# Heads' norm reordered: three centring products first, three panels of the output projection begun together, three activation table loads placed earlier

## What is computed

```python
def rwkv7_time_mix(...):                       # layer 0
    ...
    y = scan over time                         # per head of 64 columns
    mean = jnp.mean(y, axis=-1, keepdims=True)
    var = jnp.mean(jnp.square(y - mean), axis=-1, keepdims=True)
    y = ((y - mean) * lax.rsqrt(var + LNX_EPS)).reshape(B, S, BR_W) * lnx_w + lnx_b
    return y + bonus

for l in range(DEPTH):                         # DEPTH = 2
    ...
    y = concat([y_br * silu(gate),             # 768 columns
                y_mem * silu(g_mem)]) @ w_out[l]   # 256 columns; w_out is 1024 x 1024
    x = x + rms_norm(y, post_norm[l])

# second block: two feed-forward parts around a mixer, then the final norm
h = h + 0.5 * swiglu(rmsnorm(h, ffn1_norm), ...)
h = h + hybrid_mixer(rmsnorm(h, mix_norm), ...)
h = h + 0.5 * swiglu(rmsnorm(h, ffn2_norm), ...)
y = rmsnorm(h, final_norm)
```

## Time and profile before

| | before |
|---|---|
| median of 3 runs | 1286.67 us (1284.4 to 1289.2) |
| profiled execution: its own time | 1287.15 us |
| span in the profile | 1285.3 us |
| granted TensorE clock, mean | 0.978 of full speed |
| busy: PE, DVE, ACT, POOL | 93%, 66%, 49%, 15% of the span |
| DMA | 186.83 MB, 145 GB/s on average |

### The profile page before, as it was taken

How to read it: one execution, slowest core, us unless ns; L and a number is a source line. 1 busy time by engine, 2 the same in 40 slices (tenths; PEclk the granted TensorE clock), 3 DMA queues, 4 the chain that set the end, 5 groups by cost and what they waited for, 6 DMA issues and landing times.

```text
span 1285.3 us, 23942 instructions
## 1 busy us (share of the span) xinstructions
PE 1197.6 (93%) x9724; PEld 1152.2 (90%) x9724; DVE 845.7 (66%) x1456; ACT 627.4 (49%) x1079; POOL 187.6 (15%) x186
## 2 busy tenths in 40 slices
PE   5978699898996899999999999989999999999997
PEld 5978688797996799999989999879999999999996
DVE  4768854776776686654497746669556668866642
ACT  5675352664555654444343445453445445654442
POOL 1127140200002021110022000015000001212101
PEclk8989799999998999999999999999999999999999
DMA  6434210344452565555336432335454345755560
GB/s 225 130 117 132 83 67 34 98 136 145 132 164 83 177 213 179 177 159 173 115 123 190 164 132 87 110 115 196 156 179 159 120 160 168 258 185 186 169 182 33
DMA packets 53677, 186.83 MB, mean 145 GB/s; under 512 B 6720, under 2 KB 8896, under 8 KB 53184
## 3 DMA queue, kind: packets, MB, share of 16 engines
q1 hardware_dynamic: 53008, 183.07, 43.8%
q10 hardware_dynamic: 560, 2.24, 0.5%
HBM read 184.24 MB, written 1.05 MB: 144 GB/s over the span
## 4 chain that ended last, share of the span: by engine, by line
PE 75%; DVE 14%; ACT 7%; issue 3%; DMA 1%; POOL 0%; DVEq 0%; SPq 0%; ACTq 0%; POOLq 0%
PE bank L2534 20%; PE bank L2537 20%; PE bank L2535 20%; DVE wl L1979 4%; ACT wh L1607 2%; PE bank L2551 2%; PE bank L2568 2%; PE bank L2552 1%; PE bank L2555 1%; DVE sqr L2083 1%; DVE zl L2079 1%; PE bank L2577 1%; ACT L1585 1%; DVE tmp L2447 1%; DVE score L2378 1%
## 5 line engine op out<-in xcount | busy, mean ns | idle before, releaser
L1979 DVE TENSOR_TENSOR wl<-raw,wh 128x1024 fp32r<-128x1024 f32 (+1 forms) x343 | 422.5, 1240 | 206.3 <-ACT wh L1607 202.7
L2534 PE MATMUL bank<-xh,wh 128*128 128x256 f32 (+1 forms) x1880 | 544.2, 289 | 1.8 <-ACT wh L1607 1.6
L2537 PE MATMUL bank<-xh,wl 128*128 128x256 f32 (+1 forms) x1880 | 535.7, 285 | 6.9 <-DVE wl L1979 6.9
L2535 PE MATMUL bank<-xl,wh 128*128 128x256 f32 (+1 forms) x1880 | 536.7, 285 | 0.0
L1607 ACT ACTIVATE wh<-raw 128x1024 fp32r<-128x1024 f32 (+1 forms) x343 | 355.2, 1044 | 273.3 <-PE bank L2537 258.3
L2537 PEld LDWEIGHTS bank<-xh,wl 128*128 128x128 f32 x1880 | 358.4, 191 | 8.3 <-DVE wl L1979 8.3
L2534 PEld LDWEIGHTS bank<-xh,wh 128*128 128x128 f32 x1880 | 356.6, 190 | 7.3 <-issue 3.6
L2535 PEld LDWEIGHTS bank<-xl,wh 128*128 128x128 f32 x1880 | 357.4, 190 | 0.5
L2534 PE MATMUL bank<-hh,wh 128*128 128x272 f32 (+1 forms) x352 | 100.3, 285 | 0.0
L2535 PE MATMUL bank<-hl,wh 128*128 128x272 f32 (+1 forms) x352 | 100.2, 285 | 0.0
L2537 PE MATMUL bank<-hh,wl 128*128 128x272 f32 (+1 forms) x352 | 100.2, 285 | 0.0
(11 more groups left out here) (376 smaller groups left out, 1726.2 us busy)
## 6 DMA issues: line engine op xcount, KB each, us to landing
raw<-w_ffn_gate SPq DMA_DIRECT2D x44, 512.0 KB, 3.6
raw<-w_ffn_up SPq DMA_DIRECT2D x44, 512.0 KB, 3.6
raw<-w_a_w_in SPq DMA_DIRECT2D x29, 512.0 KB, 3.6
raw<-w_ffn_down SPq DMA_DIRECT2D x32, 448.0 KB, 3.4
raw<-w_w_out SPq DMA_DIRECT2D x16, 512.0 KB, 3.5
raw<-w_b_w_in SPq DMA_DIRECT2D x16, 512.0 KB, 4.6
raw<-w_ffn_down SPq DMA_DIRECT2D x16, 512.0 KB, 3.6
raw<-w_ret SPq DMA_DIRECT2D x16, 512.0 KB, 3.9
```

The lines of the kernel that those rows point to most:

```text
L1979: v.tensor_tensor(lo[:, c], raws[n % N_RAW][:, c], hi[:, c].bitcast(F32), ALU.subtract).then_inc(*w_lo.up(n))
L2534: pe.matmul(ps, hi[:, c], x_hi(k), start=(k == 0), stop=False)
L2535: pe.matmul(ps, hi[:, c], x_lo(k), start=False, stop=False)
L2537: last = pe.matmul(ps, lo[:, c], x_hi(k), start=False, stop=(k == kt - 1))
```

## The change

In layer 0 the three `norm_a` steps come first, then `norm_b(0)`, then the group of the projection's panels on tiles 6 and 7, now three panels where there were two, then `norm_b(1)`, `branch0` 0, `norm_b(2)`, `branch0` 1 and 2. The memory pair's split (`branch0` 3) moves into `step_y(1)`, behind its third tile. In layer 1 the group keeps two panels. A new step `ln_tables` loads the Ln/Exp set ahead of `mix_out(1)`, and ahead of the last projection (`down`) of each of the two feed-forward parts.

```diff
+OUT_BEGUN = (3, 2)
             def begin_out(layer, part):
-                return begin([(f"w_out{layer}", panel, f"y{layer}", S, out_evac(layer)) for panel in range(2)], part)
+                return begin([(f"w_out{layer}", panel, f"y{layer}", S, out_evac(layer)) for panel in range(OUT_BEGUN[layer])], part)
                 finish(begun)
-                for panel in range(2, KT):
+                for panel in range(OUT_BEGUN[layer], KT):
                     do("y", c, i, b, freed)
                     bank.give(b, (yd, (c, i)))
+                    if c and i == 2:
+                        do("branch0", 3)
-            do("branch0", 3)
-            da0 = norm_a(0)
-            begun = begin_out(0, (6, 7))
-            norm_b(0, da0)
-            da1 = norm_a(1)
-            norm_b(1, da1)
-            da2 = norm_a(2)
-            do("branch0", 0)
-            norm_b(2, da2)
-            do("branch0", 1)
+            centred = [norm_a(j) for j in range(3)]
+            for j, da in enumerate(centred):
+                norm_b(j, da)
+                if j:
+                    do("branch0", j - 1)
+                else:
+                    begun = begin_out(0, (6, 7))
             do("branch0", 2)
             do("branch", BT + 1)
+            do("ln_tables")
             mix_out(1, begun)
+                do("ln_tables")
                 for panel in range(KT):
                     if panel == KT - 3:
                         fewer_splits()
                     project(f"ffn{n}_down", [panel], f"hid{n}", FFN_TOK[n], down_evac, kt=FT, keep=True)
+                elif kind == "ln_tables":
+                    tables(ACT.Ln)
```

## The result

| | before | after |
|---|---|---|
| median | 1287.45 us (10 runs, 1284.1 to 1291.7) | 1292.87 us (10 runs, 1290.4 to 1295.9) |
| ratio after/before, 95% interval | | 1.0043 [1.0028, 1.0058] |
| profiled execution, its span | 1287.15, 1285.3 | 1295.35, 1293.5 |
| mean granted clock | 0.978 | 0.973 |

The changed kernel is slower by 5.4 us. The prediction was 1288.1 with a range to 1291.3, so it was 4.8 us low and the time lies outside the range.

The account below looks back on a forecast made before the run. Taken as PE-bound nearly everywhere (75% of what ended last). Norm and projection +3.5, layer 1 load -1.0, final load -1.1 gave +1.4 us: 1288.6 against the profiled 1287.15, hence 1288.1 us median; range 1283.5 to 1291.3.

Parts of the forecast that it names:

- Ln 0 early: Heads' norm, ACT: the first Ln starts at about 227.71 instead of 228.52, 0.8 us early.
- the stop inside the group until DVE's `wl2`: Heads' norm, PE: after 8 of 18 matmuls the group stands from 231.0 to 232.4, delaying the sums of pairs 1 and 2.
- the shared tiles: Layer 0 projection: three panels sharing the remaining tiles take 7.8 us instead of 9.0, giving 1.2 us back.
- the pause ahead of panel 3: Layer 0 projection: panel 3's weight split, formerly hidden by panel 2, is uncovered and costs 1.6 us.
- `mo_add` straight behind DVE's `wl`: Layer 1's projection: without the table load there, `mo_add` follows DVE's `wl` directly, winning 1.0 us.
- the final Ln: Final norm: with the table load moved, Ln starts 0.03 us behind PE's last sum, winning 1.1 us.
- The drain: Skill page's estimate: about 1380 ns more per table switch, making two loads worth up to 5.3 us; left out of the sum.
- the 3.15 us late start of tile 0: Layer 0 projection, PE: tile 0 starts at about 238.9 instead of 235.75.
- the other 10 in 1.2 us: Heads' norm, PE: the group's last ten matmuls, once `wl2` is ready, take 1.2 us, ending at 233.6.
- the clock falls earlier: Rival, chance 0.12: PE's clock drops to 1.2 GHz at 232.4, slowing ten matmuls and sum 1; 1.8 us more, 1289.9.
- Later, the same pieces shifted by 3.5: Behind the norm and projection: the program's later pieces run as before, only 3.5 us later.
- shifts here pass on one for one: Behind layer 0's projection: a shift moves everything after by the same amount, since PE works without a pause.

Follow-up runs that it names:

- run 8: The changed kernel again, unaltered, for a second profile; 1292.74 us (1 run).
- run 11: The kernel before with six more Ln of 128x512 on ACT ahead of the first head's own Ln; 1297.55 us, ratio 1.0061.
- run 15: The kernel before with two more Ln of 128x512 ahead of the first head's own; 1295.41 us, ratio 1.0051.
- run 14: The changed kernel with two begun panels, transposes filling PE's wait for the first difference head's softmax and put at the first retention head; 1286.77 us, ratio 0.9986.
- run 17: The changed kernel with two begun panels, transposes in PE's waits at the first difference head's softmax and fourth retention head's squares; 1285.89 us, ratio 0.9978.
- run 3: The changed kernel with two panels begun together instead of three; 1289.28 us, ratio 1.0008.
- run 7: The kernel before with three panels of the projection begun instead of two, no other edit; 1293.22 us, ratio 1.0037.
- run 4: The changed kernel with the third panel's weights split right behind the centring products, ahead of the first Ln; 1289.75 us, ratio 1.0013.
- run 16: The kernel before with three more Ln of 128x512 ahead of the first head's own; 1293.40 us, ratio 1.0033.
- run 2: The changed kernel with the table loads at their old places (norm change alone); 1297.31 us, ratio 1.0066.
- run 18: The changed kernel with transposes in PE's waits at the first difference head's softmax and fourth retention head's squares; 1291.40 us, ratio 1.0027.
- run 13: The changed kernel with transposes filling PE's wait for the first difference head's softmax and put at the first retention head; 1291.83 us, ratio 1.0029.

## Why the prediction was wrong, by its steps

**Right.** Ln 0 early (228.26, less the 0.41 of a late entry, for 227.7); the stop inside the group until DVE's `wl2`, and the sum of pair 1 behind it; the late Ln 1 and tile 0; the shared tiles (8.0 us from tile 0 to the group's end, for 7.8); the pause ahead of panel 3 (1.8 for 1.6); `mo_add` straight behind DVE's `wl` (1.09 for 1.0) and the final Ln 0.1 us behind the sum (1.06 for 1.1); nothing behind the first feed-forward part. The drain that the Trainium skill adds to each table load (ScalarE: Activation LUTs, What ACT_TABLE_LOAD costs) would have made 5.3 us of the loads; the profile has 2.15, and the next instruction 0.09 us behind the load at 413.23.

**Mis-sized: the 3.15 us late start of tile 0.** It measured 3.9. The failed assumption is "the other 10 in 1.2 us", at the price of the high clock. The clock was at 1.2 GHz from 230.8 to 234.2, and the ten took 1.8; `wl2` was ready at 232.92, 0.16 later than forecast once the late entry is taken off. The two make up the difference. (The first eight took 1.8 us too, where the text has 0.95, but nothing hung on them: the ninth waited for `wl2`.) It is the rival that I called "the clock falls earlier" and gave 0.12, in a smaller size: it had sum 1 at the low clock too, and that ran at 1.00. I argued against it from one window of before that stayed at 1.00 with PE little busy. The shared tiles gave back 1.0 for 1.2, the pause cost 1.8, and the stage came out at +4.7 for +3.5. These 1.2 us alone would have left the median inside the range.

**Missing: everything behind the stage.** "Later, the same pieces shifted by 3.5" and "shifts here pass on one for one" failed. This is the step that put the time outside the range. In the profiled execution the pieces behind 299 us lose another 5.3 us, 4.0 of it at two waits that the change doesn't touch; in run 8's they lose 3.9, 3.0 of it there. Neither the sum nor the range had a term for this; 0.7 us for the scatter of a median was all. Runs 11 and 15 show the same falls behind a plain delay. Run 14 shows that PE kept busy in the first wait gives 2.5 us back there. Run 17, with both waits filled, is 3.4 us under run 3; at its second wait the 1.6 us are back as well, but run 14 had them without a filling.

**Still open.** What decides whether the clock falls at a given wait. Its length alone doesn't (3.34 us before and after). Nor does the size of the shift: run 7 reached the first wait 1.1 us later than the kernel before and lost the clock there, runs 4 and 16 reached it 1.5 and 3.1 us later and didn't. That the changed kernel's falls are tied to the program, and not only more frequent in it, is not shown. That the later falls are the whole of the missing time is not shown either: filling both waits in the changed kernel gave 1.5 us, within the noise, and run 2's median is 4 us above what its stage adds (9.8 for 5.8), of which its profile shows 2.2, at 299 to 309 and behind 400 us.

## What to carry to other kernels

Beginning one more panel of a projection early is only free if its weights' split is ready: otherwise what stands behind the group in TensorE's order (here two sums, each the head of a relay through ACT and DVE) waits for it. Put the relay's sums ahead of the group, or the split ahead of both.

A few tenths of a per cent cannot be predicted for a kernel whose clock falls at waits by adding up the trace: delays of 1.4 to 4.3 us of work cost 4.2 to 7.9 us here (runs 15, 16 and 11, by their ratios). When a stage gets shorter and the median doesn't, compare the granted clock over the whole span before doubting the stage. Look at the clock of all timed executions too, and profile one of each kind: three profiles of the kernel before missed the kind that three of ten of its executions are. And a wait of some 3 us that can't be removed may be worth filling with matmuls whose results nobody reads: it gave 2.5 us at one wait of run 14, and nothing that can be told from noise in the changed kernel.

## What was not expected of the hardware

The same wait (PE idle 3.34 us) left the clock at 1.00 in three profiles of one program and at 0.5 in the first profile of another that only reaches it 5.1 us later. In the second profile of that other (run 8) the clock had already fallen at 296.4 us, ahead of the wait, so that PE came late to it and idled 1.81 us; then it fell again at 303.2:

```profile
302.53 0.55 PE L2842 MATMUL bank<-ta,scb 128*128 128x128 f32 x3 [1.81 <-DVE scb L2293]
```

Behind the first wait or the second, a low stretch of 3.4 us moved what follows by 1.4 to 1.6 us in all these profiles; the added 3.4 us of the stretch around 400 us moved it by 0.4 and 0.7 (runs 18 and 13). Sixteen transposes of 128x128 in the wait, 1.9 us of its 3.34, were enough for the clock to stay at 1.00 behind it in runs 13, 14, 17 and 18, where it falls in run 3 and the changed kernel; that the shift of the program would not have done this by itself is not shown.
